# Grouping the sample's tiles 1 | 2 | 3+4 instead of 1+2 | 3+4 for merging and routing in a two-layer mixer and PEER kernel

## The reference

```python
h = rmsnorm(x, g_attn_norm) * (1 + sc1) + sh1
# one projection of h feeds mixers A (latent attention), B (gated MLP), C (windowed attention) and three gates
merged = (gates[0] * (oa @ w_o_a) + gates[1] * (ob @ w_o_b) + gates[2] * (oc @ w_o_c))   # each D=1024 wide
x = x + g1 * (merged @ w_out)
h = rmsnorm(x, g_ffn_norm) * (1 + sc2) + sh2
q = (h @ w_pq).reshape(t, 8, 2, 128)                       # PEER: 8 heads, 2 half keys
sc = einsum('thpd,hpkd->thpk', q, keys)                    # scores against 128 keys per half
sv, si = top_k(sc, 16)                                     # 16 of 128, for each of the 16 half keys
cv, ci = top_k(sv[:, :, 0, :, None] + sv[:, :, 1, None, :], 16)   # 16 of the 256 sums
act = gelu(einsum('thkd,td->thk', u_tab[eidx], h))         # 8*16 = 128 experts per token
x = x + g2 * einsum('thk,thkd->td', softmax(cv) * act, v_tab[eidx])
```

## Time and profile before

| what | before |
|---|---|
| median of 3 runs | 5013.24 us (5009.84 to 5019.33) |
| the profiled execution | 5020.55 us, its span 5018.8 us |
| busy share of the span | PE 78%, VectorE 58%, ScalarE 33%, GpSimd 31% |
| moved by DMA | 1686.63 MB; 1342.26 MB by the gathers (65.5% of 16 engines), 340.39 MB by ordinary DMAs (17.4%) |
| chain that ended last, by engine | PE 35%, DMA 32%, DVE 20%, issue 5%, ACT 4% |
| mean granted TensorE clock | 0.866 |

### The profile page before, as it was taken

How to read it: one execution, slowest core, us unless ns; L and a number is a source line. 1 busy time by engine, 2 the same in 40 slices (tenths; PEclk the granted TensorE clock), 3 DMA queues, 4 the chain that set the end, 5 groups by cost and what they waited for, 6 DMA issues and landing times.

```text
span 5018.8 us, 62376 instructions
## 1 busy us (share of the span) xinstructions
PE 3916.2 (78%) x20334; PEld 1601.9 (32%) x20334; DVE 2904.7 (58%) x6294; ACT 1636.2 (33%) x4851; POOL 1561.1 (31%) x1453
## 2 busy tenths in 40 slices
PE   5989978888667786788699987887876777666676
PEld 3556452224222232223365333222332223211111
DVE  3543166667666568666433468666768656774544
ACT  0245012333223323333254223333333333333333
POOL 0200002333334324545101223333444422443332
PEclk8999988999778897899799988899997889876666
DMA  7100447999999999999504989999999999999998
GB/s 280 63 35 26 156 151 301 414 387 407 420 417 420 383 407 420 385 394 399 210 1 174 397 346 337 371 421 416 411 420 405 421 367 417 421 421 421 421 421 359
DMA packets 245312, 1686.63 MB, mean 336 GB/s; under 512 B 28064, under 2 KB 33760, under 8 KB 46976
## 3 DMA queue, kind: packets, MB, share of 16 engines
q0 software_dynamic: 184320, 1342.26, 65.5%
q1 hardware_dynamic: 60672, 340.39, 17.4%
HBM read 1676.90 MB, written 5.64 MB: 335 GB/s over the span
## 4 chain that ended last, share of the span: by engine, by line
PE 35%; DMA 32%; DVE 20%; issue 5%; ACT 4%; DVEq 2%; POOL 1%; SPq 0%; ACTq 0%; POOLq 0%
DMA arena<-in_experts,arena 28%; PE ps L961 11%; PE ps L1217 9%; DVE sq L1721 8%; PE ps L1168 3%; DMA arena<-in_weights 3%; PE ps L1097 2%; PE ps L1193 2%; PE ps L1122 2%; PE ps L1181 2%; DVE arena L1431 1%; PE ps L1109 1%; ACT arena L1368 1%; DMA front<-in_experts,arena 1%; DVE arena L1429 1%
## 5 line engine op out<-in xcount | busy, mean ns | idle before, releaser
L1217 PE MATMUL ps<-arena 64*64 64x512 f32 x9872 | 1642.1, 746 | 821.2 <-ACT arena L1368 792.1
L934 POOL DMA_INDIRECT arena<-in_experts,arena x1234 | 1369.9, 1110 | 2716.4 <-PE ps L1217 2167.6
L1721 DVE CUSTOM_DVE_ANT_0 sq<-arena 128x1024 f32<-128x1024 f32 x1234 | 1513.2, 1226 | 936.5 <-DMA arena<-in_experts,arena 843.4
L1217 PEld LDWEIGHTS ps<-arena 64*64 64x64 f32 x9872 | 325.0, 151 | 1878.1 <-issue 1838.5
L1362 ACT ACTIVATE arena<-arena 128x1 f32<-128x1 f32 x1280 | 257.8, 201 | 2040.1 <-DVE arena L1721 2039.2
L961 PE MATMUL ps<-arena 128*128 128x512 f32 (+3 forms) x1920 | 853.7, 586 | 41.5 <-DMA arena<-in_weights 27.6
L1368 ACT ACTIVATE arena<-ident,arena 128x128 f32<-128x128 f32 x1280 | 513.9, 401 | 92.5 <-issue 5.1
L961 PEld LDWEIGHTS ps<-arena 128*128 128x128 f32 x1920 | 359.2, 199 | 540.2 <-issue 489.0
L1364 ACT ACTIVATE arena<-arena 128x1 f32<-128x1 f32 x1280 | 376.9, 294 | 89.9 <-issue 2.4
L1193 PE MATMUL ps<-arena 128*128 128x256 f32 (+1 forms) x1536 | 351.7, 374 | 6.2 <-issue 5.8
L1193 PEld LDWEIGHTS ps<-arena 128*128 128x128 f32 x1536 | 258.4, 200 | 183.6 <-issue 151.1
(11 more groups left out here) (174 smaller groups left out, 3035.8 us busy)
## 6 DMA issues: line engine op xcount, KB each, us to landing
arena<-in_weights SPq DMA_DIRECT2D x263, 1024.0 KB, 9.4
arena<-in_experts,arena POOLq DMA_INDIRECT x1234, 15.3
arena<-mod_rows SPq DMA_DIRECT2D x26, 512.0 KB, 9.0
arena<-in_weights SPq DMA_DIRECT2D x20, 576.0 KB, 8.1
arena<-in_weights SPq DMA_DIRECT2D x10, 768.0 KB, 9.2
arena<-in_weights SPq DMA_DIRECT2D x15, 512.0 KB, 7.9
arena<-in_g_norm SPq DMA_DIRECT2D x9, 512.0 KB, 16.1
arena<-in_keysT SPq DMA_DIRECT2D x4, 1024.0 KB, 9.1
```

The costliest lines, as they stand in the source:

```text
L934: nc.gpsimd.indirect_dma_start(out=ring[BUF[n]], out_offset=None, in_=ins["experts"], in_offset=bass.IndirectOffsetOnAxis(ap=index(t)[:, s ...
L1217: last = MM(acc[h][to:to + 64, :], diag[n % 4][lo:lo + 64, lo:lo + 64], ring[BUF[n]][lo:lo + 64, D + c * 512:D + (c + 1) * 512], start=s = ...
L1721: V.tensor_tensor_reduce(out=sq[:], in0=ring[BUF[n]][:, 0:D], in1=h2_of_slot(n), scale=1.0, scalar=0.0, op0=ALU.mult, op1=ALU.add, accum_o ...
```

## The change

The group (1, 2) becomes two groups, (1,) and (2,); (3, 4) stays and is now group 3. Ahead of stage 0 only tile 1 is merged and routed; tile 2 moves into the line, with its second top-k woven into its `route`. In stage 1 tiles 1 and 2 go one after the other. The positions in both lines are set anew: tiles 3 and 4 are merged at 90 to 190 (was -4 to 165) in stage 0 and at 150 to 246 (was 118 to 320) in stage 1, where the prompt's items come 65 to 73 slots earlier. Row buffer 4 serves in stage 0 up to slot 180, so `gains` and `rope` are loaded again at 192 for the prompt's first part; 6 opens only behind the last half query of group 3.

```diff
-GROUPS = {0: (0,), 1: (1, 2), 2: (3, 4)}
+GROUPS = {0: (0,), 1: (1,), 2: (2,), 3: (3, 4)}
@@ schedule(), stage 0 @@
-    line.spread(-4, 165, pieces(merge(0, 2) + route(0, 2)))
-    line.spread(12, 100, choose(0, 2))
-    line.spread(160, 215, mod_items(1))
-    line.spread(170, 235, choose(0, 3))
-    line.spread(205, 262, pieces(norm_and_inputs(0, (0,), ())))
-    line.spread(264, 280, prompt_attention(0) + [("rows2", 0, 0), ("consts", 1)])
-    line.put(292, [("scaled", 1)])
+    line.spread(-4, 90, pieces(merge(0, 2) + route(0, 2, 2)))
+    line.spread(90, 190, pieces(merge(0, 3) + route(0, 3)))
+    line.spread(192, 240, choose(0, 3))
+    line.spread(160, 210, mod_items(1))
+    line.put(192, [("consts", 1)])
+    line.put(203, [("scaled", 1)])
+    line.spread(208, 262, pieces(norm_and_inputs(0, (0,), ())))
+    line.spread(264, 280, prompt_attention(0) + [("rows2", 0, 0), ("consts", 2)])
+    line.put(292, [("scaled", 2)])
@@ schedule(), stage 1 @@
-    line.spread(-3, 118, pieces(merge(1, 1) + route(1, 1, 1)))
-    line.spread(140, 236, choose(1, 2))
-    line.spread(118, 320, pieces(merge(1, 2) + route(1, 2)))
-    line.put(316, [("consts", 2)])
-    line.put(328, [("scaled", 2)])
-    line.spread(322, 372, choose(1, 3))
-    line.spread(330, 400, pieces(norm_and_inputs(1, (0,), ())))
-    line.spread(402, 420, prompt_attention(1) + [("rows2", 1, 0)])
-    line.spread(422, 490, pieces(merge(1, 0) + route(1, 0)))
-    line.spread(390, 460, choose(1, 4))
-    line.spread(500, 560, choose(1, 0))
+    line.spread(-3, 40, pieces(merge(1, 1)))
+    line.spread(40, 78, pieces(route(1, 1, 1)))
+    line.spread(78, 150, pieces(merge(1, 2) + route(1, 2, 2)))
+    line.spread(150, 246, pieces(merge(1, 3) + route(1, 3)))
+    line.put(250, [("consts", 3)])
+    line.put(258, [("scaled", 3)])
+    line.spread(262, 340, choose(1, 3))
+    line.spread(262, 335, pieces(norm_and_inputs(1, (0,), ())))
+    line.spread(337, 355, prompt_attention(1) + [("rows2", 1, 0)])
+    line.spread(357, 425, pieces(merge(1, 0) + route(1, 0)))
+    line.spread(390, 450, choose(1, 4))
+    line.spread(455, 520, choose(1, 0))
@@
-RELEASE = [{6: ("pq", 0, 1, 15), 8: ("o", 0, 4, 1)},
-           {6: ("pq", 1, 1, 15), 7: ("pq", 1, 0, 15), 8: ("o", 1, 4, 1), 9: ("n2", 1, 0), 10: ("sc", 1, 0, 15)}]
-UNTIL = [{4: 0, 6: 388, 7: 0, 9: 0, 10: 0}, {4: 306}]
+RELEASE = [{6: ("pq", 0, 3, 15), 8: ("o", 0, 4, 1)},
+           {6: ("pq", 1, 3, 15), 7: ("pq", 1, 0, 15), 8: ("o", 1, 4, 1), 9: ("n2", 1, 0), 10: ("sc", 1, 0, 15)}]
+UNTIL = [{4: 180, 6: 388, 7: 0, 9: 0, 10: 0}, {4: 238}]
@@ places of the half queries and scores: room for three tiles instead of two @@
-            return at(17408 + 256 * (q % 2), 256)
+            return at(17408 + 384 * (q % 2), 384)
-            return at(17920 + 256 * (q % 2), 256)
+            return at(18432 + 384 * (q % 2), 384)
@@ SyncE, "consts" @@
                     if l == 1:
+                        sp.wait_ge(slot_used, FINAL_IN[0, 4] + 1)
+                        sp.dma_start(rope, ins["rope"]).then_inc(masks_in, 16)
+                    elif l == 2:
                         sp.wait_ge(*ready("om", 0, 0, 1))
-                    elif l == 2:
+                    elif l == 3:
                         sp.wait_ge(slot_used, FINAL_IN[1, 4] + 1)
-                    sp.dma_start(gains, to_all(row("gains", min(l, 1)))).then_inc(consts_in, 16)
+                    sp.dma_start(gains, to_all(row("gains", l // 2))).then_inc(consts_in, 16)
...
@@ VectorE, "scaled" @@
                     dve.wait_ge(consts_in, 32 * (l + 1))
+                    if l:
+                        dve.wait_ge(masks_in, 48)
```

## The result

| what | before | after |
|---|---|---|
| median | 5016.28 us (4 runs, 5009.84 to 5023.93) | 5161.06 us (4 runs, 5157.08 to 5166.85) |
| ratio | 1 | 1.0289 (95% interval 1.0270 to 1.0308) |
| span of the profiled execution | 5018.8 us | 5157.1 us |
| moved by DMA | 1686.63 MB | 1750.59 MB |
| mean granted TensorE clock | 0.866 | 0.854 |

The account below looks back on a forecast made before the run. DMA at 421 GB/s was taken to bound the expert slots, except dense stretches bound by TensorE or VectorE and a serial part ahead of stage 0. -106 + 129 + 115 = +138 us gave 5151 us, range 5055 to 5200.

Parts of the forecast that it names:

- The start: Ahead of stage 0: merging and routing one tile saves 106 us, first slot from 779 to about 673 us.
- The route: Ahead of stage 0: with one tile its four rounds get shorter, saving 35 us with the second tile's transposes.
- The merge: Ahead of stage 0: merging one tile takes 77 us, not 153.9, saving 77 us before 6 charged for weights.
- The forecast stall: Start of the merge ahead of stage 0: weights queue behind 3.1 MB of rows and keys; 6 us charged.
- The merge's DMA share: Ahead of stage 0, a sign to look for: DMA share near 0.95 in the one-tile merge.
- Segments of stage 0: Slots 0 to 190, each segment priced by its largest engine: 720 us against 593, +127; whole stage +129.
- The factor 1.15: Routes with turns: VectorE's summed work times 1.15 for engines waiting on each other; 1.0 would give 76 us less.
- Segments of stage 1: Merges and routes up to slot 246, priced by the largest engine: 957 us; whole stage 2413 against 2298, +115.
- The last 343 slots: End of stage 1: 343 slots at 2.55 us each, 875 us against 712 before.
- the second rival: Both stages: density losses stay as before, only bytes are added; +46 us, 5059 us; 18 in 100.
- the first rival: Stage 1: DMA's unused time carries 71 of 75 us of weights; -25 us, 4988 us; 6 in 100.
- the third rival: Ahead of stage 0, three weight units starve one tile, 19 us; stages' row buffers add 15; +172, 5185 us; 10 in 100.

Follow-up runs that it names:

- experiments 3: Changed kernel with the 60 weight loads of tile 2's own group cut to an eighth of their columns; 5120.93 us, 1.0197 to the kernel before.
- experiment 4: Changed kernel with layer 1's tiles 3 and 4 merged and routed over slots 150 to 320, not 246, later positions as before; 5114.41 us, 1.0189.
- experiment 6: Changed kernel with the turns of tile 2's second top-k moved from its route beside the merge of tiles 3 and 4; 5151.71 us, 1.0261.
- experiment 5: Changed kernel with row buffer 6 opened behind group 2's last half query, not group 3's; 5160.47 us against 5159.68 of the changed kernel.
- experiment 9: Kernel before with only layer 0 regrouped, tile 2's turns beside the merge of tiles 3 and 4, that merge and route over slots 88 to 206; 5039.18 us, 1.0041.
- experiment 11: Kernel before with stage 1's tiles 1 and 2 merged and routed over slots -3 to 125, not -3 to 118; 5008.52 us, 0.9972.
- experiment 8: On a kernel with only layer 0 regrouped and stage 0 thinned, keys and modulation rows loaded behind the first blocks' weights; 5062.10 us, 1.0091.

## Why the prediction was right

It was 10 us under the measured median, on the right side. Three of the 10 us are the median before, 5016.28 us with a fourth run where the prediction had 5013.24; 7 are the sum, 138 against 145. The mechanism holds: serial time goes, bytes come, and dense places cost beyond the bytes. The closeness is in part luck, since errors of the parts, from -13 to +19 us, cancelled.

- **The start** gave 100 us, not 106. The route came as forecast: from the last `o` matmul to the first slot 100 us and not 136. The merge was mis-sized: 91 us instead of 154, so 63 saved where 77 - 6 were counted. The forecast stall of 6 us was 11, of which 3 are the lower clock behind it, and two waits just ahead of `o` take 3 (TensorE idle for 1.7 and 1.2 us), where the kernel before has one of 0.9. The merge's DMA share, a sign that was to be near 0.95, was 0.77.
- **Segments of stage 0** came to 153, 154, 244 and 160 us; forecast 158, 167, 235 and 160. The factor 1.15, taken from a route with two tiles' top-k, is too high for the route of one tile over 48 slots: 154 us against VectorE's bare 145, 1.06. It is too high in stage 1 as well: 140 us against 131 (1.07) and 145 against 129 (1.12). The merge of tiles 3 and 4 was undersized by 4%: TensorE was busy for 233 of its 244 us.
- **Segments of stage 1** came to 163, 140, 140, 145, 235 and 130 us from its first slot on, 953 in all; forecast 154, 150, 142, 149, 233 and 129, 957. In the first DMA was full (1.01): the 160 us of its window are 64 slots or units at 421 GB/s, and 62 were counted. From 246 to 425 it took 600 where I had 581. That is not `choose(1, 3)` beside the prompt's norms (slots 262 to 335, first row): DMA is full there. It is low in the prompt's attention (slots 335 to 357, second row):

```profile
3730.00:3955.00 225.00, 156.54 (x755) 48.65 (x748) 149.59 (x293) 73.86 (x240) 99.40 (x91) 0.81 1.01 416
3955.00:4026.00 71.00, 47.96 (x288) 20.94 (x292) 38.15 (x67) 38.35 (x113) 24.39 (x23) 0.74 0.82 322
```

  The kernel before had the same dip, at 0.81 over slots 400 to 420, so it explains none of the difference. The stretch moves 3 MB (8 us) more than the nine added slots account for; the rest is open. The last 343 slots took 867, forecast 875.
- **Bytes or density** (the second rival, 5059 us): experiments 3 and 4 part them. Taking away seven eighths of tile 2's loads is worth 40 to 46 of 131 us, thinning one merge 50 us. The rival is refuted for these positions; with tiles 3 and 4 thinned (experiment 4) stage 1 pays 68 us, close to its 75.
- **Idle DMA time carries the weights** (the first rival): refuted, 5161 us against 4988. The routes with turns that were to run at DMA's pace ran at 0.89 to 0.97 of its share. That VectorE's work in them is what held them is shown by experiments 3 (less DMA work, same length) and 6 (turns out, shorter).
- **The ring can't feed one tile** (the third rival): 11 us ahead of stage 0 and, by experiment 5, nothing where tiles 3 and 4 are merged.
- The Trainium skill's rule in "DMA: Bandwidth & Descriptors", section "Where 436 GB/s comes from", that the HBM side binds at about 358 GB/s between HBM and SBUF, was left aside for the trace's 421 GB/s. The trace after does not agree with it either: one-tile merges held 421 and 415 GB/s.

What stays open: whether the later prompt's part or `choose(0, 3)` cost experiment 9 more, the 4 us that it lost behind slot 390 with no more bytes, and why, in experiment 6, stage 0 kept so little of its 12 us.

## What to carry to other kernels

When weights are streamed once per group of tiles, a smaller group ahead of the first use pays only for what is serial: price the serial time that goes against the reload's bytes and, above all, against where the work goes, since a stage that looks DMA-bound on average is bound by TensorE or VectorE wherever the work per slot exceeds the slot's 2.5 us. Add up the three engines per slot for each stretch, thin the stretch that exceeds DMA, and count what it pushes behind it; a dense stretch is best lengthened over slots that have nothing else, as the one changed number of experiment 11 did.

## What the runs showed of the hardware that was not expected

- A merge in which TensorE is busy for 228 of 235 us still took in some 32 us of VectorE's top-k for 5 us more, while a route took 15 us for the 16 us of them that fell in it (experiment 6).
- A wait of TensorE can cost more than its length. Behind 8 us of idle time ahead of stage 0 the granted clock was 0.50 for 6 us, and a block of 16 matmuls took 10.12 us instead of 6.87. In experiment 8 a block behind a wait of 3.16 us took 8.80 us.
- Ordinary loads put in another order brought nothing: one wait of 7.0 us on weights became two of together 4.9, and the first slot came no earlier (experiment 8).
